# A two-layer hybrid backbone on one core: router, output gates, one adaLN group and the size of the expert units

## The reference

```python
logits = xt @ w_router                      # 8 experts
top_v, top_i = lax.top_k(logits, 2)
top_w = softmax(top_v)
out = sum over e of gate[:, e] * swiglu(xt, wg[e], wu[e], wd[e])   # hidden width 2816
```

## Time and profile before

| | us |
|---|---|
| median of 3 runs | 1752.93 (1750.93 to 1757.45) |
| the profiled execution's own time | 1756.52 |
| its span, first to last instruction | 1754.7 |
| TensorE busy | 1646.6 (94%) |
| TensorE loading weights (beside it) | 1469.8 (84%) |
| VectorE busy | 532.1 (30%) |
| ScalarE busy | 300.5 (17%) |
| moved by DMA | 408.94 MB, mean 233 GB/s |

### The profile page before, as it was taken

One profiled execution on the slowest core, in us unless ns is written; L12 is line 12 of the kernel. 1 busy time (PEld: TensorE's weight loads), 2 busy tenths in 40 slices (PEclk: granted clock), 3 DMA queues, 4 the chain that ended last, 5 costly groups with the idle time before them and its releaser, 6 DMA issues.

```text
span 1754.7 us, 59240 instructions
## 1 busy us (share of the span) xinstructions
PE 1646.6 (94%) x27345; PEld 1469.8 (84%) x27345; DVE 532.1 (30%) x1257; ACT 300.5 (17%) x695; POOL 16.4 (1%) x32
## 2 busy tenths in 40 slices
PE   5999898999979999999489999999999999999996
PEld 3887588997457888989379999999999999999995
DVE  1464226767272446664613101000000101000001
ACT  2112322011024223433123000010101000010001
POOL 1000000000000000000000000000000000000000
PEclk9999999999999999999797999999999999999998
DMA  9723858545492310000444999999899999999880
GB/s 356 257 97 104 300 199 266 173 168 183 159 305 62 109 50 5 7 6 5 172 164 158 352 369 348 348 358 377 333 366 353 354 365 349 357 353 362 330 320 25
DMA packets 175312, 408.94 MB, mean 233 GB/s; under 512 B 13106, under 2 KB 86244, under 8 KB 175076
## 3 DMA queue, kind: packets, MB, share of 16 engines
q1 hardware_dynamic: 170480, 398.91, 63.0%
q0 software_dynamic: 1184, 3.41, 0.6%
q10 hardware_dynamic: 3412, 2.93, 0.5%
HBM read 403.30 MB, written 1.92 MB: 231 GB/s over the span
## 4 chain that ended last, share of the span: by engine, by line
PE 46%; PEld 43%; DVE 4%; issue 3%; ACT 2%; DMA 1%; SPq 0%; DVEq 0%; PEldq 0%; POOL 0%; ACTq 0%
PEld bank L1404 27%; PEld bank L1425 13%; PE bank L952 8%; PE bank L985 4%; PE bank L629 3%; PE bank L626 3%; PE bank L729 2%; PE bank L732 2%; PE bank L1164 2%; PE bank L1124 2%; PE bank L754 2%; PE bank L1160 2%; PE bank L1100 2%; PE bank L1149 2%; PE bank L652 2%
## 5 line engine op out<-in xcount | busy, mean ns | idle before, releaser
L1404 PEld LDWEIGHTS bank<-w,ring 128*64 128x64 f32 x11264 | 468.2, 137 | 18.9 <-issue 18.2
L1404 PE MATMUL bank<-w,ring 128*64 128x96 f32 x11264 | 477.2, 246 | 3.3 <-issue 2.7
L1425 PE MATMUL bank<-w,ring 128*64 128x96 f32 x5632 | 240.6, 247 | 2.7 <-issue 2.5
L1425 PEld LDWEIGHTS bank<-w,ring 128*64 128x64 f32 x5632 | 235.8, 138 | 5.9 <-issue 5.0
L2702 DVE TENSOR_TENSOR w<-w,bank 128x384 f32<-128x384 f32 (+1 forms) x48 | 23.6, 519 | 622.2 <-PE bank L1404 622.2
L1898 ACT ACTIVATE w<-bank 128x384 f32<-128x384 f32 (+1 forms) x48 | 20.5, 462 | 462.1 <-PE bank L1404 462.0
L626 PE MATMUL bank<-w,ring 128*128 128x256 f32 x256 | 57.7, 387 | 5.9 <-DVE w L2380 5.4
L626 PEld LDWEIGHTS bank<-w,ring 128*128 128x128 f32 x256 | 49.5, 194 | 14.2 <-DVE w L2380 5.6
L629 PE MATMUL bank<-ring,w 128*128 128x256 f32 x256 | 58.1, 391 | 0.9 <-DVE w L1962 0.9
L652 PE MATMUL bank<-ring,ct 128*32 128x256 f32 x768 | 48.3, 403 | 10.0 <-DMA ring<-in_ada_w 6.2
L629 PEld LDWEIGHTS bank<-ring,w 128*128 128x128 f32 x256 | 50.2, 197 | 8.5 <-DVE w L1962 1.3
(11 more groups left out here) (427 smaller groups left out, 1979.1 us busy)
## 6 DMA issues: line engine op xcount, KB each, us to landing
ring<-in_moe_w_gate SPq DMA_DIRECT2D x88, 1024.0 KB, 6.3
ring<-in_moe_w_up SPq DMA_DIRECT2D x88, 1024.0 KB, 6.8
ring<-in_moe_w_down SPq DMA_DIRECT2D x88, 1024.0 KB, 6.5
ring<-in_ada_w SPq DMA_DIRECT2D x48, 1024.0 KB, 6.0
ring<-in_ev_w_in SPq DMA_DIRECT2D x11, 1024.0 KB, 13.4
ring<-in_ffn_w_gate SPq DMA_DIRECT2D x11, 1024.0 KB, 7.8
ring<-in_ffn_w_up SPq DMA_DIRECT2D x11, 1024.0 KB, 5.4
ring<-in_ffn_w_down SPq DMA_DIRECT2D x11, 1024.0 KB, 6.5
```

The costliest lines, as they stand in the source:

```text
L1404: ins = [mm(b[hp, (a % 4) * CAP:(a % 4 + 1) * CAP], w[:, k, a * P + hp.start:a * P + hp.stop], XG[:, kk, :], start=kk == 0 and a % 4 == 0, ...
L1425: ins = [mm(bank[4 + c // 4][hp, (c % 4) * CAP:(c % 4 + 1) * CAP], w[:, k, c * P + hp.start:c * P + hp.stop], HIDU[:, s % 2, 2 * part + k, :],
```

## The change

Four things change. The router's product now has 32 columns of router weights as the stationary operand and all 256 tokens moving, for each of the 8 feature chunks, on four column strips in turn; the four strips are added and brought to tokens by a second small product with a constant (`C_STRIP`), and it follows `HT` chunk by chunk. The choice of experts does the scans and selections of both sets back to back. Group 11's tiles come before `rw_g2` and `rw_w_o` in the ring, and its products, copy, turn and sums are in pair 0 of the recurrence. `gates(2)` is made and copied before VectorE's normalisation of y is over, `gates(3)` behind the output projection, and squares and gating of `O` go tile by tile (`take_out`, `gated_tiles`, `root_of_parts`), as in the even layer. `CAP` becomes 88.

```diff
-CAP = 96
+CAP = 88
...
-N_ODD_OUT = N_V + 5
-N_ADA3 = N_ODD_OUT + 4
-N_MOE = N_ADA3 + ADA_TILES + 1
+N_ADA3 = N_V + 4
+N_G2 = N_ADA3 + ADA_TILES
+N_ODD_OUT = N_G2 + 1
+N_MOE = N_ODD_OUT + 4 + 1
...
-EXPERTS = FREE[4:] + ROUND[4:] + ROUND[:3] + FREE[:4] + ROUND[3:4]
+EXPERTS = FREE + ROUND[2:] + ROUND[:2]
...
+    c[:, C_STRIP:C_STRIP + NE] = row % 32 == np.arange(NE)[None, :]
...
             for n in range(4):
                 tile([cols(t["rw_w_v"][0], n * TW)])
+            ada_group(11)
             tile([whole(0, 1024, t["rw_g2"][0])])
             for n in range(4):
                 tile([cols(t["rw_w_o"][0], n * TW)])
+            tile([(lambda s: s[:, 0:KC * NE].rearrange("p (k n) -> p k n", k=KC), kp(t["moe_router"][0]))])
             sp.wait_ge(sem("y"), 2 * KC)
             sp.wait_ge(sem("trk_done"), KC)
-            ada_group(11)
-            tile([(lambda s: s[:, 0:KC * NE].rearrange("p (k n) -> p k n", k=KC), kp(t["moe_router"][0]))])
...
                 z(i, 3)
+                if i == 0:
+                    pe.wait_ge(sem("v_copied"), 3)
+                    ada_part(11, 0)
...
                 z(i, 4)
+                if i == 0:
+                    ada_part(11, 1)
...
                 xp(i, 5)
+                if i == 0:
+                    turn_mods(11)
...
+            pe.wait_ge(sem("so"), KC)
+            gates(2)
+            pe.wait_ge(sem("gb_copied"), 12)
             pe.wait_ge(sem("proj_copied"), PROJ_ODD + 23 + 4)
             pe.wait_ge(sem("yg"), 1)
             turn(lambda c, st: Y1[:, c, st, :], 4)
             pe.wait_ge(sem("mt"), 2)
             for n in range(4):
                 tile_product(YG1, False)
-            pe.wait_ge(sem("so"), KC)
-            gates(2)
-            pe.wait_ge(sem("gb_copied"), 12)
-            ada_group(11)
+            gates(3)
...
-            for st in range(NST):
-                for k in range(KC):
-                    ins = mm(bank[4][:, st * NE:(st + 1) * NE], HT[:, k, st * P:(st + 1) * P], w[:, k, :],
-                             start=k == 0, stop=k == KC - 1)
+            for k in range(KC):
+                pe.wait_ge(sem("ht0"), 3 * KC + k + 1)
+                pe.wait_ge(sem("ht1"), 3 * KC + k + 1)
+                q = k % 4
+                ins = mm(bank[4][32 * q:32 * q + 32, 0:TW], w[:, k * NE:k * NE + 32], HT[:, k, :], start=k < 4, stop=k >= 4)
...
-            pe.wait_ge(sem("route"), 1)
-            gates(3)
+            turned_back(0)
+            pe.wait_ge(sem("lge"), 1)
+            for st in range(NST):
+                ins = mm(bank[7][:, st * NE:(st + 1) * NE], LOGITS[:, st * P:(st + 1) * P],
+                         CST[:, C_STRIP:C_STRIP + NE], start=True, stop=True)
+            ins.then_inc(sem("routed"), 1)
+            turned_back(1)
...
                     take(G1[:, st, h * 512:(h + 1) * 512], None)
+            act.wait_ge(sem("stored_rwkv"), 32 * KC)
+            copy_gates(2)
             act.wait_ge(sem("var"), 3)
             A(SM[:, 128:160], SM[:, 128:160], ACT.Sqrt).then_inc(sem("var_root"), 1)
             for n in range(4):
-                take(O[:, :, n * TW:(n + 1) * TW], N_ODD_OUT + n, src=halves)
-            act.wait_ge(sem("proj_copied"), proj[0])
-            norm_o()
-            act.wait_ge(sem("stored_rwkv"), 32 * KC)
-            copy_gates(2)
-            norm_x(3, lambda: take_sums(11))
+                take_out(N_ODD_OUT, n)
+            root_of_parts(3)
+            act.wait_ge(sem("gated"), 6)
+            copy_gates(3)
+            norm_x(3)
             modulated(5, 2, 1)
-            act.wait_ge(sem("route"), 3)
-            A(SM[:, 60:62], SM[:, 60:62], ACT.Exp).then_inc(sem("lge"), 1)
+            act.wait_ge(sem("routed"), 1)
+            A(LOGITS, bank[4][:, 0:TW], ACT.Copy).then_inc(sem("lge"), 1)
             for n in range(4):
                 act.wait_ge(sem("htm_done"), n + 1)
                 A(HTM[:, n // 2, (n % 2) * 512:(n % 2 + 1) * 512], bank[n][:, :], ACT.Copy).then_inc(sem("htm"), 1)
-            act.wait_ge(sem("x"), 6)
-            copy_gates(3)
+            act.wait_ge(sem("route"), 3)
+            A(SM[:, 60:62], SM[:, 60:62], ACT.Exp).then_inc(sem("lge"), 1)
...
-            gated(2)
+            gated_tiles(2, PROJ_ODD + 23 + 8)
             residual(2)
             normed_x()
             modulated(5, 2, 1)
-            mods(11)
...
+            v.tensor_scalar(IOTA1, IOTA[:, 0:CAP], 1.0, None, ALU.add).then_inc(made("dve_chain"), 1)
+            dve.wait_ge(sem("routed"), 2)
             L = SM[:, 100:116]
-            v.tensor_copy(L, bank[4][:, 0:16]).then_inc(made("route"), 1)
+            v.tensor_copy(L, bank[7][:, 0:16]).then_inc(made("route"), 1)
...
```

More of the change, by code:

```diff
@@ L87, in slot_of @@
         return m % RING
-    if m < N_ADA3:
+    if m < N_MOE:
         return ROUND[(m - N_V) % 6]
-    if m < N_MOE - 1:
-        return FREE[m - N_ADA3]
-    if m == N_MOE - 1:
-        return ROUND[3]
     return EXPERTS[(m - N_MOE) % RING]
 def tile_before(m):
-    return N_V + 3 if m == N_MOE - 1 else m - 6 if N_V <= m < N_ADA3 else m - RING
+    return m - 6 if N_V <= m < N_MOE else m - RING
 def ada_taken(n):
@@ L255, in ada_sums @@
                 return W[2][:, n * TW:(n + 1) * TW]
+            if n == 11:
+                return ring[:, FREE[3], 1536:1536 + TW]
             return W[3][:, 1536 + (n % 2) * TW:1536 + (n % 2 + 1) * TW]
         def sums_bank(n):
-            return bank[(4, 5, 6, 6, 6, 6, 4, 5, 0, 1, 4, 6)[n]]
+            return bank[(4, 5, 6, 6, 6, 6, 4, 5, 0, 1, 4, 7)[n]]
         def even_bank(p):
@@ L367, in program @@
         HTM = W[2][:, :].rearrange("p (s n) -> p s n", s=NST)
+        LOGITS = W[5][:, 1024:1280]
+        IOTA1 = W[5][:, 1280:1280 + CAP]
         ROUTE = W[3]
@@ L1195, in solve @@
                         pe.wait_ge(sem("so"), i)
+                    else:
+                        pe.wait_ge(sem("mod"), 12)
                 for j in range(4):
```

46 lines of the change are left out of this document (23 added, 23 removed).

## The result

The changed kernel takes 1730.72 us (median of 4 runs, 1727.71 to 1737.35). Beside it the kernel before takes 1754.12 (4 runs, 1750.93 to 1757.45). The ratio is 0.9872 with an interval of 0.9836 to 0.9908. The forecast was 1694.3, 36 us less. The profiled execution took 1737.35 us, its span is 1735.5; it is the slowest of the four, so times read from its trace add up to less of a gain than the medians.

What follows compares the result with a forecast made beforehand. It took TensorE's moving columns to bound the expert units, after a serial chain. Terms of -3.2 us up to the first expert product and -55.4 for units made -58.6, so 1694.3 against the median; range 1689 to 1701.

Steps and rivals of the forecast that it cites:

- part 6: Expert stage, units of 88 tokens: 3.28 ns less a record over 16896 records, -55.4 us (bounds -47 and -58).
- The lead of 21 us: Expert units: 28 us from a slot's release to its next use, 6.3 for transfer; the rest absorbs shortfalls.
- Part 1: adaLN group 11 moved into pair 0 of the recurrence: +3.3 us, between 0 and 4.3.
- Part 2: Early output gates: ScalarE's copies wait for the last state's store ahead of the Sqrt, +6.7 us (+0.3 to +10).
- Parts 3 to 5: Output projection to experts: squares and gating by tile -5.0, router on strips -4.9, shorter choice and gates(3) moved -3.3 us.
- T: The end of the output projection's last product, 906.1 us in the kernel before.
- A: Rival: the state stores ahead of the experts land early, the early gates cost 0.3 us, 1688 us; chance 0.12.
- B: Rival: half clock stays; gather 2 us longer, up to 4 us lost in the first unit, 1700 us; chance 0.10.
- C: Rival: weight loads share the pitch in the expert units, so narrower units gain 0, 1750 us; chance 0.04.
- The estimate of 1732: Time from the Trainium skill's slope of 0.13 ns a column, 17.6 us for the units in place of 55.4.
- D: Rival: transfers become the bound, no unit below 97.5 us, TensorE waits for them, 1722 to 1743 us; chance 0.07.
- E: Rival: an expert with more than 88 tokens needs a ninth unit of 91.5 us, 1786 us; chance 0.03.

Runs made afterwards that it cites:

- c5: The changed kernel loading only half of each expert tile (half the k blocks, all 128 partitions) from unit 1 on; 1688.54 us, ratio 0.9629.
- c7: The changed kernel with half of each expert tile loaded from unit 1 on and units of 96 tokens; 1740.75 us, ratio 0.992.
- c9: The changed kernel loading three quarters of each expert tile, all 128 partitions, from unit 1 on; 1693.43 us, ratio 0.9653.
- d1: The changed kernel with all expert bytes loaded, but TensorE multiplying only every other k block; 1643.67 us, ratio 0.9356.
- c2: The changed kernel with 264 semaphore increments that nobody waits for added to each unit on TensorE; 1900.78 us, ratio 1.0838.
- a4: The changed kernel with ScalarE's Sqrt ahead of its wait for the stored states and the gate copies; 1733.79 us, ratio 0.987.
- a2: The changed kernel with units of 96 tokens (CAP = 96); 1753.01 us, ratio 0.9983.

## Why the prediction was wrong

**The step that failed** is in part 6: "A unit becomes 91.5 us and asks for 378 GB/s, under the 403 shown". Both halves of the sentence are true of the tiles and neither reaches the instructions. I took the pitch of the records and the rate of the transfers as all that can set a unit. In the changed kernel 128 records execute in 4.9 us (38.3 to 38.5 ns each). Their instructions come in packets of 16 KB; where TensorE had to wait, it started again 1.4 us after a packet's end, and each packet takes 1.0 us itself. While the experts' tiles keep the DMA engines busy for 0.98, the packets come every 5.6 us in the median. At 41.8 ns a record 128 of them took 5.35 us, and most of this was hidden: before, a unit lost 1.6 us (98.43 against 96.81 with half loads), and the change to 88 tokens raised the loss to 5.5 to 7 us (95.2 to 96.9 against 89.75). The measured unit is 95.2 to 96.9 us after the first; the term of -55.4 us became 785.8 - 768.8 = -17.0.

c5, c7 and c9 show that without the DMA engines' load the loss is not there; the 38 of 39 gaps show that it is a wait for instructions, and d1 that it isn't one for tiles. c2 shows that the load is not the only thing that can bring such waits about. What the trace doesn't show is when TensorE asks for a packet. That the packet waits in line behind the tiles' packets is argued from its late start and the busy share, and not shown itself.

The lead of 21 us, "absorbs shortfalls", was right for tiles: their last part lands 19 to 25 us ahead of use in all units but the first. It made me sure of the wrong resource. The trace of the kernel before had a small sign. TensorE has 8 gaps of over 0.25 us in the expert stage, 4.5 us in all, and 7 of them end 1.2 to 1.65 us behind a packet. The 18.2 us of waits of the weight loads for "issue", which are easier to see, are not a sign: c5 has 17.8 in the same row and loses nothing.

**Part 1** was right within its bounds: +3.3 forecast, and at most 4.3. From ScalarE's last copy ahead of pair 0 (line 1711, 605.80) to the first store of a state (678.11) it is 72.3 us in the kernel before. In the changed kernel (line 1724, 603.79, to 679.85) it is 76.1: +3.7, and these two lengths are the same within 0.02 us in every trace of either order of the tiles. But the profiled execution of the changed kernel came to this place 2.0 us earlier. The profiled executions of the changed kernel and of its variants, alike up to there, came between 603.5 and 606.6, so this says nothing of the change. So the last copy of y starts at 847.07 in place of 845.36, only 1.7 later. The other 2.0 us are luck.

**Part 2** was right. The Sqrt starts at 864.02 in place of 855.50: 8.5 later, 1.7 of it there already at the copy of y, so +6.8 for +6.7. The store landed 11.3 us after its issue, and a4 took this price off again.

**Parts 3 to 5.** T is 884.27 + 30.03 = 914.30. The turn starts at 922.42, T + 8.1 (T + 8.3 forecast). VectorE's timeline in the changed kernel, answering to the earlier trace rows:

```profile
929.64 0.17 DVE L2618 COPY sm<-bank 128x16 f32<-128x16 f32 x1 [0.59 <-PE bank L1367]
...
932.01 0.17 DVE L2640 TENSOR_TENSOR w<-sm 128x16 f32<-128x16 f32 x1
```

The logits are read 7.2 us behind the turn's start (8.2 forecast), and CHOSEN is made 2.5 us later (forecast 2.55). From the read to the first product it is 12.8 us where I had 11.9: the gather takes 7.14 us for 5.42, which was the bound of "+2". (The prediction gave a mean clock of 0.8 for the gather before; over its own 5.42 us the granted clock was 0.69, and now it is 0.50.) The sum to the first product was T + 28.4 and is T + 28.2: parts 4 and 5 missed by 1.0 and 0.9 us in opposite ways. In all the first product moves by -5.3 us, forecast -3.2. Without the 2.0 us of luck ahead of pair 0 it is -3.3.

**The rivals.** A didn't happen. B did in part: the gather at the half clock costs 1.7 us, and the first 256 records of the first unit take 11.93 us for the 9.93 of the next ones, as the clock is at its lower level until 946.6. C is refuted: 9.81 us for 256 records, and 52 us for 8 columns when the rest allows it (c7 to c5). The estimate of 1732 that stands beside C lies 1.3 us from the measured time by chance: it came from 0.13 ns a column, and from 96 to 88 columns a record went from 41.8 to 38.3 ns, 0.44 ns a column. D had the right sum for the wrong reason; it named the transfers as the bound, and what it looked for, waits of TensorE for tiles, isn't there. E didn't happen: 88 loads of each matrix as before.

**Behind the units**, in the profiled execution, the last eight scatter records take 6.88 us (3.71 before). The changed kernel's chain of waits has them:

```profile
1714.27 6.88 PE bank L1399 x8
```

Over these 6.88 us the granted clock was 0.53, where it was 1.00 over the same records before. And the window over their end has the clock at 0.50, its lower level:

```profile
1718.00:1735.00 17.00, 3.13 (x4) 0.67 (x2) 7.15 (x9) 3.77 (x6) 1.07 (x2) 0.50 0.16 62
```

So the span's account is -5.3 to the first product (2.0 of it luck), -17.0 in the units and +3.1 behind them: -19.2, from 1754.7 to 1735.5. The medians differ by 23.4; the trace is of the slowest of the changed kernel's executions, and the other 4 us are in none of these terms.

## What to carry to other kernels

A long stream of short instructions has a supply of its own. Before costing a shorter instruction, look for gaps of the engine itself, put down to "issue", that end the same short time behind the landing of an instruction packet (1.2 to 1.65 us here). In the kernel before they were some 4 us in all, which was the whole warning; waits of the weight loads for "issue" and the time between packets were about the same with and without a shortage. In this kernel units of 88 tokens lost at most 1.4 us with the DMA engines busy for 0.90, and 5.5 to 7 us at 0.98 to 0.99; added semaphore increments brought the shortage on at 0.83. A gain ahead of such a stage may be gone behind it (a2, a4). And to test whether load on the DMA engines is a cause, shorten the transfers and keep their form: check the busy share, not the bytes.

## What the runs showed of the hardware that I had not expected

- A packet of 16,384 bytes carries 256 of TensorE's instructions. It took 1.0 us, and TensorE started again 1.2 to 1.65 us after it had landed, in 38 of the changed kernel's 39 gaps of over 0.25 us.
- Loads into 96 partitions moved 231 GB/s at a busy share of 1.00; loads into 128 partitions 290 GB/s at 0.90 for the same number of bytes, and 399 GB/s for whole tiles.
- 264 semaphore increments between TensorE's products cost 18 to 24 us a unit, 70 to 90 ns each. Some two thirds of it were waits for instruction packets, at a DMA busy share of 0.83.
- A small store issued when 5 MB of loads were queued landed after 11.3 us, where the median of such stores before was 2.4 us.
